# A hybrid encoder trunk on one core: experts gathered in pairs from split halves, the router per token tile, and identity products in TensorE's gaps

## The chip, the cores and the metric

The kernel runs on one core of one Trainium2 chip. The metric is the device time of one execution in microseconds (us), and a kernel's time is the median of its runs. The profile is one more execution, with its own time.

## The reference

The input is 256 tokens of 1024 float32 values. After a layer norm come two layers. Each is a token mixer (retention, S5, Hyena and mLSTM head groups), a residual and a norm, then a SwiGLU channel mixer, a residual and a norm. The channel mixer is dense in the first layer; in the second each token goes to the best two of eight experts:

```python
def moe_swiglu(x, router, w1, w3, w2):
    logits = (xt @ router).astype(jnp.float32)
    top_val, top_idx = lax.top_k(logits, TOP_K)      # TOP_K = 2 of N_EXPERTS = 8
    gate = jax.nn.softmax(top_val, axis=-1)
    combine = jnp.einsum("tk,tke->te", gate, jax.nn.one_hot(top_idx, N_EXPERTS))
    ...
    # out = sum over experts e of combine[:, e] * swiglu(xt, w1[e], w3[e], w2[e])
```

An expert has 3584 hidden columns (`w1`, `w3`: 1024 x 3584, `w2`: 3584 x 1024), so the weights of all eight are 352 MB and are read once.

## The kernel before, in words

The program is written out by hand for each engine. Semaphores tie the engines together, and each engine works in the order of its text. The tokens are two tiles of 128 (`h[:, t, :]`). The order around the change is: token mixer of layer 1 (`mix_1`), `layer_norm(3)` on DVE, transposes of the normed `h` on PE (`transposes_of_h(3)`, tile 1 first) into `hT` (ACT, `evacuate_h`), the router, the experts, `layer_norm(4)` and the output.

**Layer norm.** DVE computes the mean and variance of a tile, GpSimd (POOL) the power -1/2 (L500), DVE scales (L1484, L1490). PE stands still from the last product of the mixer until the first tile is normed.

**Router.** PE waits until all of `hT` is there, makes the logits (L1022, 16 products of 8 columns), DVE selects the best two (L2019 to L2035), PE counts places with products against a triangle and against ones (L1027 to L1031), and DVE turns them into `posx`, the place of each token in each expert's list of up to 128 tokens (L2044 to L2047).

**Experts.** One after the other, each in 14 chunks (`NC_E`) of 256 hidden columns, 112 chunks in all. Chunk `g` has 2 MB of `w1`, `w3` and 1 MB of `w2`, in a ring of four slots that SyncE (SP) fills: it issues the load of `w1`, `w3` (L374) when PE has finished `up` of the chunk that had the slot, and that of `w2` (L378) after `down`. The products are made from float32 data split into a high and a low part of the type fp32r (hi*hi, lo*hi, hi*lo; `SPLIT`). For a chunk ACT writes the high half of the weights (`split_up`, L1353, two pieces into one buffer `ex_up_hi`; L1449 for `w2`), DVE the low half (`up_lo`, L1962; `w2_lo`, L2086), PE makes `up` (L1075, 24 products of 512 columns), two transposes and `down` of the chunk before (L1096, 12 products of 512).

**An expert's tokens.** `prepare` (DVE, L2052) writes the one-hot matrix `pick_x`; `gather` (PE, L1039) multiplies `h`, plain float32, by it, 16 products of 128 columns in two halves, for one expert; `take_x` (ACT, L1408) and `x_lo` (DVE, L2069) split the result into `ex_x`, of which there are two. `placing` (L1046) transposes `pick_x` for the way back, `scatter` (L1059) and `add` (L2063) bring the result to the tokens. For expert x+1 this is done during chunks 7 to 11 of expert x: DVE writes `pick_x` in its chunk 7, PE gathers after chunks 8 and 9, `add` for the expert before is in DVE's chunks 4 and 6. Of a float32 product that is no transpose the trace has two records; of an fp32r product and of a transpose it has one.

A branch repeats all experts if one has more than 128 tokens; it isn't taken in the profile.

## Time and profile before

| | |
|---|---|
| median of 3 runs | 1730.88 us (1726.97 to 1731.34) |
| the profiled execution: its time, its span | 1726.48 us, 1724.6 us |
| PE matmul busy | 1650.9 us, 96% |
| DVE busy | 1353.5 us, 78% |
| ACT busy | 944.0 us, 55% |
| POOL busy | 56.4 us, 3% |
| mean granted TensorE clock | 0.958 |
| chain that ended last, by engine | PE 84%, DVE 10%, ACT 4% |

The clock is a share of 2.4 GHz; it is granted at 1.00 (2.4 GHz) or 0.50 (1.2 GHz). "PE L1075" is TensorE's matmul at line 1075. The experts are the stretch from 709.9 to 1707 us.

### The profile page before, as it was taken

What the parts mean: (1) busy time and instruction counts of PE and PEld (TensorE: products, weight loads), DVE (VectorE), ACT (ScalarE), POOL (GpSimd) and SP (SyncE); (2) the same over time, 40 slices, a digit from 0 to 9 for tenths busy, and PEclk for the clock granted to TensorE, in tenths of its full rate; (3) what the DMA queues carried; (4) which work ended last, traced back from release to release, by engine and by line L of the source; (5) the groups of instructions that cost most, each with busy time, mean ns of one, the idle gap of its engine ahead of it and who ended that gap; (6) DMA issues with size and microseconds to landing.
All of it is one profiled execution on the core that took longest, in us unless ns stands there. A gap on an engine that the chain in (4) does not pass through costs nothing.

```text
span 1724.6 us, 18678 instructions
## 1 busy us (share of the span) xinstructions
PE 1650.9 (96%) x7674; PEld 1306.7 (76%) x7674; DVE 1353.5 (78%) x1443; ACT 944.0 (55%) x943; POOL 56.4 (3%) x39
## 2 busy tenths in 40 slices
PE   6998989999999998899999999999999999999995
PEld 4665748988858764788888888888888888888883
DVE  6879456765665945598898998888988989888996
ACT  4312315654310232477777776777777767777772
POOL 0111000000011100000000000000000000000000
PEclk9978989999998978799999999999999999999997
DMA  7221152743433114598988998998989989989870
GB/s 311 98 98 49 74 212 86 270 182 147 173 145 147 49 73 182 208 371 344 375 351 339 372 353 346 366 362 337 364 348 354 361 356 356 360 330 374 350 305 26
DMA packets 40459, 444.23 MB, mean 258 GB/s; under 512 B 4400, under 2 KB 4528, under 8 KB 7216
## 3 DMA queue, kind: packets, MB, share of 16 engines
q1 hardware_dynamic: 39216, 438.78, 65.2%
q10 hardware_dynamic: 1152, 4.19, 0.6%
q8 instruction: 62, 1.02, 0.2%
q14 instruction: 29, 0.24, 0.0%
HBM read 437.71 MB, written 5.24 MB: 257 GB/s over the span
## 4 chain that ended last, share of the span: by engine, by line
PE 84%; DVE 10%; ACT 4%; issue 1%; DMA 0%; DVEq 0%; SPq 0%; ACTq 0%
PE bank L1075 33%; PE bank L1096 15%; PE bank L981 7%; PE bank L583 4%; PE bank L990 3%; PE bank L800 3%; PE bank L587 3%; PE bank L1039 2%; PE bank L753 1%; PE bank L1083 1%; DVE ring_lo L1962 1%; DVE ring_lo L2086 1%; ACT ex_up_hi L1353 1%; PE bank L726 1%; PE bank L1059 1%
## 5 line engine op out<-in xcount | busy, mean ns | idle before, releaser
L1962 DVE TENSOR_TENSOR ring_lo<-ring,ex_up_hi 128x2048 fp32r<-128x2048 f32 x224 | 512.8, 2290 | 50.9 <-ACT ex_up_hi L1353 50.7
L1353 ACT ACTIVATE ex_up_hi<-ring 128x2048 fp32r<-128x2048 f32 x224 | 429.1, 1916 | 115.7 <-PE bank L1075 108.0
L1075 PE MATMUL bank<-ex_up_hi,ex_x_hi 128*128 128x512 f32 x896 | 363.0, 405 | 3.7 <-DVE ring_lo L1962 3.7
L1075 PE MATMUL bank<-ring_lo,ex_x_hi 128*128 128x512 f32 x896 | 350.6, 391 | 0.0
L1075 PE MATMUL bank<-ex_up_hi,ex_x_lo 128*128 128x512 f32 x896 | 349.7, 390 | 0.0
L2086 DVE TENSOR_TENSOR ring_lo<-ring,ex_w_hi 128x2048 fp32r<-128x2048 f32 x112 | 255.5, 2282 | 1.4 <-ACT ex_w_hi L1449 1.4
L1449 ACT ACTIVATE ex_w_hi<-ring 128x2048 fp32r<-128x2048 f32 x112 | 213.4, 1905 | 0.0
L1075 PEld LDWEIGHTS bank<-ex_up_hi,ex_x_hi 128*128 128x128 f32 x896 | 168.3, 188 | 40.9 <-DVE ring_lo L1962 10.8
L1075 PEld LDWEIGHTS bank<-ring_lo,ex_x_hi 128*128 128x128 f32 x896 | 168.2, 188 | 36.2
L1075 PEld LDWEIGHTS bank<-ex_up_hi,ex_x_lo 128*128 128x128 f32 x896 | 168.8, 188 | 30.5
L1096 PE MATMUL bank<-ex_w_hi,ex_mid_hi 128*128 128x512 f32 x448 | 174.4, 389 | 2.1 <-DVE ex_mid_lo L2080 2.1
L1096 PE MATMUL bank<-ring_lo,ex_mid_hi 128*128 128x512 f32 x448 | 174.3, 389 | 0.0
L1096 PE MATMUL bank<-ex_w_hi,ex_mid_lo 128*128 128x512 f32 x448 | 174.3, 389 | 0.0
L981 PE MATMUL bank<-ff_x_hi,ff_up_hi 128*128 128x256 f32 x352 | 102.1, 290 | 3.5 <-DVE ff_up_lo L1968 3.5
L981 PE MATMUL bank<-ff_x_lo,ff_up_hi 128*128 128x256 f32 x352 | 100.7, 286 | 0.0
L981 PE MATMUL bank<-ff_x_hi,ff_up_lo 128*128 128x256 f32 x352 | 100.6, 286 | 0.0
L1096 PEld LDWEIGHTS bank<-ex_w_hi,ex_mid_hi 128*128 128x128 f32 x448 | 84.1, 188 | 19.7 <-DVE ring_lo L2086 2.3
L1096 PEld LDWEIGHTS bank<-ring_lo,ex_mid_hi 128*128 128x128 f32 x448 | 84.1, 188 | 17.5
L1096 PEld LDWEIGHTS bank<-ex_w_hi,ex_mid_lo 128*128 128x128 f32 x448 | 84.1, 188 | 17.4
L2080 DVE TENSOR_TENSOR ex_mid_lo<-bank,ex_mid_hi 128x256 fp32r<-128x256 f32 x112 | 47.4, 424 | 61.5 <-ACT ex_mid_hi L1419 61.5
L583 PE MATMUL bank<-hT,win 128*128 128x256 f32 x384 | 88.9, 391 | 2.2 <-ACT hT L1146 1.5
L1444 ACT ACTIVATE sc<-bank 128x256 f32<-128x256 f32 x112 | 43.0, 384 | 86.1 <-PE bank L1075 86.1
(316 smaller groups left out, 2187.7 us busy)
## 6 DMA issues: line engine op xcount, KB each, us to landing
ring<-moe SPq DMA_DIRECT2D x112, 2048.0 KB, 7.6
ring<-moe SPq DMA_DIRECT2D x112, 1024.0 KB, 7.6
ring<-ffn SPq DMA_DIRECT2D x11, 3072.0 KB, 10.9
win<-w_in SPq DMA_DIRECT2D x12, 2048.0 KB, 8.6
win<-w_out SPq DMA_DIRECT2D x4, 2048.0 KB, 10.4
lnb<-ln SPq DMA_DIRECT2D x4, 1024.0 KB, 6.1
tab<-yT ACTq DMA_DIRECT2D x8, 512.0 KB, 5.6
pr<-par SPq DMA_DIRECT2D x2, 1728.0 KB, 12.2
```

The costliest lines, as they stand in the source:

```text
L583: ins = mm(b[:, q * L:(q + 1) * L], w[:, k, c:c + P], hT[:, k, :], start=(k == 0), stop=(k == KT - 1))
L587: ins = mm(b[:, :], hT[:, k, part * P:(part + 1) * P], w[:, k, :], start=(k == 0), stop=(k == KT - 1))
L800: ins = mm(bank[b][:, :], yT[:, k, t * P:(t + 1) * P], w[:, k, :], start=(n == 0 and i == 0), stop=(n == 3 and i == 1))
L981: ins = mm(bank[4 + u % 2][:, w * L:(w + 1) * L], ff_up[j][:, w, k, :], ff_x[i][:, k, :], start=(k == 0 and n == 0), stop=(k == KT - 1 and ...
L990: ins = mm(bank[2 * t + hf][:, :], ff_mid[i][:, u % 2, t * P:(t + 1) * P], ff_w2[j][:, hf * 512:(hf + 1) * 512], start=False, stop=(u == N ...
L1075: ins = mm(b[:, :], ex_x[x % 2][x_][:, k, :], (ex_up_hi, lo)[w_][:, k, :], start=(k == 0 and m == 0), stop=(k == KT - 1 and m == 2))
L1096: ins = mm(bank[2 * (x % 2) + hf][:, :], ex_mid[a][:, g % 2, f * P:(f + 1) * P], w2[b], start=(c == 0 and f == 0 and m == 0), stop=(c == N ...
L1353: act(ex_up_hi[:, HS * q:HS * (q + 1), :], wt[:, HS * q:HS * (q + 1), :], ACT.Copy).then_inc(e_uh, 1)
L1449: act(ex_w2_hi[g % 2][:, :], ring[here][:, UPW:SLOT], ACT.Copy).then_inc(e_wh, 1)
L1962: tt(ring_lo[s][:, half], ring[s][:, half], hi.bitcast(F32), ALU.subtract).then_inc(e_ul, 1)
L2080: tt(ex_mid[1][:, g % 2, :], bank[4 + g % 2][:, 0:L], ex_mid[0][:, g % 2, :].bitcast(F32), ALU.subtract).then_inc(e_mid, 1)
L2086: tt(ring_lo[s][:, UPW:SLOT], ring[s][:, UPW:SLOT], ex_w2_hi[g % 2][:, :].bitcast(F32), ALU.subtract).then_inc(e_wl, 1)
```

## The change

1. **Gather in pairs, split.** `pick_x` holds the one-hot matrices of two experts (256 columns). `h` is split beforehand into `h_hi` (ACT, in `keep_h`) and `h_lo` (POOL, L511 of the changed kernel), both fp32r, and a gather for a pair is 32 products of 256 columns in four quarters of 8. `ex_x` gets a third buffer. For the pair of experts x+1, x+2 (x odd) DVE writes `pick_x` in chunk 6, PE gathers after chunks 7 to 10, ACT and DVE split in chunks 8 to 11 in pieces of 256 columns. The first pair is gathered half before and half inside the first `up`.
2. **Router.** The logits of a tile are made as soon as its half of `hT` is there; the comparisons are written over both tiles at once; the gates and the test for more than 128 tokens come after the first `prepare`; the places are released before the totals. `h` times alpha, the start value of `acc`, is made per tile next to `h_hi`.
3. **Identity products.** `keep_busy(n, bank)` issues n products of the identity with itself (float32, 128 columns, so two records each) into a PSUM bank that nobody uses then: 10 before the first transposes, 18 before those of norm 1, 22 before and 6 between those of norm 3, and 4, 12 and 6 in the router.
4. The load of the last norm's weights (`load_ln(4)`) moves behind expert 5 on SP, since `ex_x2` lies over `lnb`.

```diff
@@ ex_x, h_hi, h_lo, pick_x
-                for i, a in enumerate(("cv", "pr"))]
+                for i, a in enumerate(("cv", "pr", "lnb"))]
+        h_hi = [over_sb("h_hi0", "yT", D, [P, D]), over_sb("h_hi1", "cst", CONST["pos"][0], [P, D])]
+        h_lo = over_sb("h_lo", "h", 0, [P, TT, D])
-        pick_x = over_sb("pick_x", "sc", 1024, [P, TT, P])
+        pick_x = over_sb("pick_x", "sc", 1024, [P, TT, 2 * P])
@@ gpsimd, after the norm's powers
+                if n == 3:
+                    for i, t in enumerate(TILES[n]):
+                        po.wait_ge(q_res, i + 1)
+                        po.wait_ge(q_hi, i + 1)
+                        nc.gpsimd.tensor_tensor(h_lo[:, t, :], h[:, t, :], h_hi[t][:, :].bitcast(F32), ALU.subtract
+                                                ).then_inc(q_lo, 1)
@@ tensor
+            def keep_busy(count, b):
+                for _ in range(count):
+                    mm(bank[b][:, 0:P], ident, ident, start=True, stop=True)
@@ transposes_of_h
                 for i, t in enumerate(TILES[n]):
+                    if n == 3 and i:
+                        keep_busy(6, 7)
                     pe.wait_ge(h_ready, 2 * n + i + 1)
@@ the order of PE's text
             pe.wait_ge(s_id, 16)
+            keep_busy(10, 7)
             transposes_of_h(0)
             mix_0()
+            keep_busy(18, 7)
             transposes_of_h(1)
             dense()
             transposes_of_h(2)
             mix_1()
+            keep_busy(22, 7)
             transposes_of_h(3)
-            pe.wait_ge(ht_ready, 16)
-            for t in range(TT):
+            for i, t in enumerate(TILES[3]):
+                if i:
+                    keep_busy(4, 4)
                 for k in range(KT):
+                    if k % HS == 0:
+                        pe.wait_ge(ht_ready, 12 + 2 * i + k // HS + 1)
                     ins = mm(bank[6][:, t * NE:(t + 1) * NE], hT[:, k, t * P:(t + 1) * P], rw[:, k, :], ...
             ins.then_inc(q_lg, 1)
+            keep_busy(12, 4)
             pe.wait_ge(q_sel, 1)
...
+            keep_busy(6, 4)
-            def gather(x, q):
-                pe.wait_ge(e_p, x + 1)
-                for i in range(4):
-                    k = 4 * q + i
+            def gather(m, q):
+                if q == 0:
+                    pe.wait_ge(e_p, m + 1)
+                elif q >= 2:
+                    pe.wait_ge(e_xg, 4 * m + q - 1)
+                for i in range(2):
+                    k = 2 * q + i
                     for t in range(TT):
-                        ins = mm(bank[6 + q][:, i * P:(i + 1) * P], h[:, t, k * P:(k + 1) * P],
-                                 pick_x[:, t, :].bitcast(F32), start=(t == 0), stop=(t == 1))
+                        for n, part in enumerate((h_hi[t], h_lo[:, t, :])):
+                            ins = mm(bank[6 + q % 2][:, i * 2 * P:(i + 1) * 2 * P], part[:, k * P:(k + 1) * P],
+                                     pick_x[:, t, :], start=(t == 0 and n == 0), stop=(t == 1 and n == 1))
@@ up
                     for k in range(HS * q, HS * (q + 1)):
+                        if g % CH == 0 and k in (2, 4):
+                            gather(x // 2, k // 2 + 1)
@@ scalar
+            def keep_h(t):
+                act(h_hi[t][:, :], h[:, t, :], ACT.Copy).then_inc(q_hi, 1)
+                act(acc[:, t, :], h[:, t, :], ACT.Copy, scale=ALPHA).then_inc(q_res, 1)
@@ evacuate_h
+                    if n == 3 and i:
+                        keep_h(TILES[3][0])
@@ vector
+            def prepare(m):
+                e = 2 * m % NE
+                tt(pick_x[:, :, :].rearrange("p t (i s) -> p t i s", i=2), bc(bc(K("iota"), 1, 2), 1, TT),
+                   bc(posx[:, :, e:e + 2], 3, P), ALU.is_equal).then_inc(e_p, 1)
@@ DVE's chunks (x odd)
-                        if c == 7:
+                        if c == 6:
                             ve.wait_ge(e_tm, x + 1)
-                            prepare(x - x0 + 1)
-                        if c in (9, 10):
-                            x_lo(x + 1, c - 9)
+                            prepare((x + 1) // 2)
+                        if 8 <= c < 12:
+                            x_lo((x + 1) // 2, c - 8)
```

PE's order from the transposes of norm 3 to the first expert, before: `cst,h` is a transpose of `h`, `pr,hT` the router, `vo,cst` the counting of places, `pick_x,h` the gather.

```order
L514 MATMUL bank<-cst,h 128x128 x16
L1022 MATMUL bank<-pr,hT 128x8 x16
L1027 MATMUL bank<-vo,cst 128x8
L1028 MATMUL bank<-vo,cst 128x8
L1029 MATMUL bank<-vo,cst 128x8
L1030 MATMUL bank<-vo,cst 128x8
L1031 MATMUL bank<-vo,cst 128x8
L1039 MATMUL bank<-pick_x,h 128x128 x16
```

And in the changed kernel, where L522 is the identity product and L1068 the gather:

```order
L522 MATMUL bank<-cst 128x128 x22
L532 MATMUL bank<-cst,h 128x128 x8
L522 MATMUL bank<-cst 128x128 x6
L532 MATMUL bank<-cst,h 128x128 x8
L1045 MATMUL bank<-pr,hT 128x8 x8
L522 MATMUL bank<-cst 128x128 x4
L1045 MATMUL bank<-pr,hT 128x8 x8
L522 MATMUL bank<-cst 128x128 x12
```

Both tiles' transposes stand ahead of the first router products, and the 4 and 12 identity products stand between and behind the router's; 6 more stand between the counting and the gather.

DVE's order over chunk 6 and 7 of an odd expert, before (`ret` is `add`, `ring_lo<-ring,ex_up_hi` half of the next chunk's low weights):

```order
L2086 TENSOR_TENSOR ring_lo_68<-ring,ex_w_hi_58 128x2048
L2063 SCALAR_TENSOR_TENSOR ret<-bank,vo,ret 128x512 x2
L1962 TENSOR_TENSOR ring_lo_66<-ring,ex_up_hi 128x2048
L2121 TENSOR_TENSOR sc<-sc,bank 128x256
L1962 TENSOR_TENSOR ring_lo_66<-ring,ex_up_hi 128x2048
L2080 TENSOR_TENSOR ex_mid_lo<-bank,ex_mid_hi 128x256
L2086 TENSOR_TENSOR ring_lo_65<-ring,ex_w_hi_57 128x2048
L2052 TENSOR_SCALAR pick_x<-cst,vo 128x128 x2
```

And in the changed kernel:

```order
L2132 TENSOR_TENSOR ring_lo_66<-ring,ex_w_hi_58 128x2048
L2106 SCALAR_TENSOR_TENSOR ret<-bank,vo,ret 128x512 x2
L2095 TENSOR_TENSOR pick_x<-cst,vo 128x512
L2009 TENSOR_TENSOR ring_lo_68<-ring,ex_up_hi 128x2048
L2171 TENSOR_TENSOR sc<-sc,bank 128x256
```

The one-hot matrix, now 512 columns in one instruction, has moved into the chunk that also has `add`, ahead of the low weights that PE takes next.

## Rows read from the trace of the kernel before

**Rows 1.** The page: PE's busy time, and the DMA engines' busy tenths in 40 slices

```profile
PE 1650.9 (96%) x7674; PEld 1306.7 (76%) x7674; DVE 1353.5 (78%) x1443; ACT 944.0 (55%) x943; POOL 56.4 (3%) x39
...
DMA  7221152743433114598988998998989989989870
```

**Rows 2.** Groups by line, 590 us to the end: count | busy us, mean ns | idle before <-releaser

```profile
L1353 ACT ACTIVATE ex_up_hi<-ring 128x2048 fp32r<-128x2048 f32 x224 | 429.1, 1916 | 115.7 <-PE bank L1075 108.0 <-PE bank L800 7.7
L1075 PE MATMUL bank<-ex_up_hi,ex_x_hi 128*128 128x512 f32 x896 | 363.0, 405 | 3.7 <-DVE ring_lo L1962 3.7
...
L1039 PE MATMUL bank<-pick_x,h 128*128 128x128 f32 x256 | 33.4, 288 | 1.4 <-DVE pick_x L2052 1.4
...
L2069 DVE TENSOR_TENSOR ex_x_lo<-bank,ex_x_hi 128x512 fp32r<-128x512 f32 x16 | 11.0, 685 | 6.2 <-ACT ex_x_hi L1408 6.2
...
L1408 ACT ACTIVATE ex_x_hi<-bank 128x512 fp32r<-128x512 f32 x16 | 9.5, 593 | 9.2 <-PE bank L1039 9.2
```

**Rows 3.** SP's issues in expert 1, one at the end of each chunk's `up`

```profile
898.54 0.33 SPq L374 DMA_DIRECT2D ring<-moe  x1
...
906.95 0.33 SPq L374 DMA_DIRECT2D ring<-moe  x1
...
917.16 0.33 SPq L374 DMA_DIRECT2D ring<-moe  x1
```

**Rows 4.** Timeline of PE in the dense stage: start us, length us

```profile
300.07 0.28 PE L981 MATMUL bank<-ff_x_hi,ff_up_hi 128*128 128x256 f32 x1
300.19 0.28 PE L981 MATMUL bank<-ff_x_lo,ff_up_hi 128*128 128x256 f32 x1
```

**Rows 5.** Timeline of DVE in chunk 6 of expert 1

```profile
888.86 1.40 DVE L2063 SCALAR_TENSOR_TENSOR ret<-bank,vo,ret 128x512 f32<-128x512 f32 x2
890.18 2.28 DVE L1962 TENSOR_TENSOR ring_lo<-ring,ex_up_hi 128x2048 fp32r<-128x2048 f32 x1
```

**Rows 6.** Timeline of PE: the first product of chunk 7 of expert 1

```profile
892.55 0.46 PE L1075 MATMUL bank<-ex_up_hi,ex_x_hi 128*128 128x512 f32 x1
```

**Rows 7.** Timeline of all engines, norm 3 to the second chunk [idle before <-releaser]

```profile
687.75 4.49 DVE L1962 TENSOR_TENSOR ring_lo<-ring,ex_up_hi 128x2048 fp32r<-128x2048 f32 x2
...
690.54 6.99 PE L1022 MATMUL bank<-pr,hT 128*128 128x8 f32 x32 [0.69 <-ACT hT L1146]
697.57 0.17 DVE L2019 COPY vo<-bank 128x16 f32<-128x16 f32 x1 [5.34 <-PE bank L1022]
...
699.13 0.29 DVE L2031 TENSOR_TENSOR vo<-vo 128x128 f32<-128x128 f32 x1
...
703.74 6.18 PE L1039 MATMUL bank<-pick_x,h 128*128 128x128 f32 x32 [1.38 <-DVE pick_x L2052]
...
714.92 1.28 ACT L1444 ACT_TABLE_LOAD   x1
...
720.78 0.49 PE L1075 MATMUL bank<-ex_up_hi,ex_x_hi 128*128 128x512 f32 x1 [0.23 <-DVE ring_lo L1962]
```

**Rows 8.** Timeline of all engines: a subtraction on DVE beside an addition on POOL

```profile
144.16 2.35 POOL L493 TENSOR_TENSOR ring<-ring 128x1024 f32<-128x1024 f32 x1 [8.32 <-DVE ring L1818]
...
145.50 1.56 DVE L1645 TENSOR_TENSOR lnb<-lnb 128x512 f32<-128x512 f32 x1
```

**Rows 9.** Stretches: length, busy (count) of PE, PEld, DVE, ACT, POOL, PEclk, DMA

```profile
679.90:684.80 4.90, 0.05 (x1) 0.00 (x0) 4.76 (x9) 3.71 (x2) 1.49 (x2) 1.00 0.82 291
...
690.50:697.60 7.10, 6.99 (x32) 6.90 (x32) 1.76 (x2) 0.00 (x0) 0.00 (x0) 0.50 0.99 420
```

**Rows 10.** Stretch of the same view in the mixer of layer 1

```profile
548.30:551.70 3.40, 3.40 (x19) 3.40 (x18) 0.00 (x0) 0.33 (x1) 0.00 (x0) 0.50 1.01 429
```

**Rows 11.** Timeline of PE: products of 16 columns in the mixer of layer 1

```profile
543.93 3.73 PE L593 MATMUL bank<-pr,hT 128*128 128x16 f32 x32
```

**Rows 12.** Timeline of PE and DVE at norm 1

```profile
255.03 1.97 PE L514 MATMUL bank<-cst,h 128*128 128x128 f32 x8 [5.29 <-DVE h L1490]
...
260.44 1.29 DVE L1985 TENSOR_TENSOR ff_x_lo<-bank,ff_x_hi 128x512 fp32r<-128x512 f32 x2 [0.48 <-ACT ff_x_hi L1146]
```

More of the change, by code:

```diff
@@ L445, in _ @@
                 load_first(c)
-            load_ln(4)
             def load_chunk(g):
@@ L1033, in gather @@
-            def gather(x, q):
-                pe.wait_ge(e_p, x + 1)
-                for i in range(4):
-                    k = 4 * q + i
+            mm(bank[5][:, 0:NE], K("before"), sel[:, 0, :], start=True, stop=True)
+            mm(bank[5][:, NE:2 * NE], K("ones"), sel[:, 0, :], start=True, stop=False)
+            mm(bank[5][:, NE:2 * NE], K("before"), sel[:, 1, :], start=False, stop=True).then_inc(q_pos, 1)
+            mm(bank[3][:, 0:NE], K("ones"), sel[:, 0, :], start=True, stop=False)
@@ L1105, in all_experts @@
                 x0 = b * NE
-                gather(x0, 0)
-                gather(x0, 1)
-                placing(x0)
+                pe.wait_ge(q_lo, TT)
+                for q in range(2):
+                    gather(x0 // 2, q)
                 for i in range(CH):
@@ L1427, in all_experts @@
                         split_up(q, MOE_SLOTS[CH % SLOTS])
-                take_x(x0, 0)
-                take_x(x0, 1)
+                for q in range(4):
+                    take_x(x0 // 2, q)
                 for i in range(CH):
@@ L1436, in all_experts @@
                         mid_hi(g - 1)
-                    if c in (9, 10) and x < x0 + NE - 1:
-                        take_x(x + 1, c - 9)
+                    if 8 <= c < 12 and x % 2 and x < x0 + NE - 1:
+                        take_x((x + 1) // 2, c - 8)
                     if more:
@@ L2017, in _ @@
             ve.wait_ge(q_lg, 1)
-            ve.wait_ge(mix_ready, 4)
             link(nc.vector.tensor_copy(lg, bank[6][:, 0:16].rearrange("p (t e) -> p t e", t=2)))
+            other, own = bc(lg, 2, NE), bc(lg, 3, NE)
+            tt(cmp1, other, own, ALU.is_gt)
+            link(tt(cmp2, other, own, ALU.is_equal))
+            link(tt(cmp2, cmp2, bc(K("lower").rearrange("p (a b) -> p a b", a=NE), 1, TT), ALU.mult))
+            link(tt(cmp1, cmp1, cmp2, ALU.add))
+            link(nc.vector.tensor_reduce(rt[3], cmp1, AX.X, ALU.add))
@@ L2020, in _ @@
+            ts(sel, rt[3], 1.5, None, ALU.is_lt).then_inc(q_sel, 1)
+            ve.wait_ge(q_sel, 1)
+            ts(rt[4], sel, -4096.0, 4096.0, ALU.mult, ALU.add)
             link(nc.vector.tensor_reduce(rt1[:, 0:2], lg, AX.X, ALU.max))
             tt(el, lg, bc(rt1[:, 0:2], 2, NE), ALU.subtract).then_inc(q_l, 1)
-            for t in range(TT):
-                a, b = bc(lg[:, t, :], 1, NE), bc(lg[:, t, :], 2, NE)
-                tt(cmp1[:, t], a, b, ALU.is_gt)
-                ins = tt(cmp2[:, t], a, b, ALU.is_equal)
@@ L2027, in _ @@
-            link(ins)
-            for t in range(TT):
-                ins = tt(cmp2[:, t], cmp2[:, t], K("lower").rearrange("p (a b) -> p a b", a=NE), ALU.mult)
-            link(ins)
-            link(tt(cmp1, cmp1, cmp2, ALU.add))
-            for t in range(TT):
-                ins = nc.vector.tensor_reduce(rt[3][:, t, :], cmp1[:, t], AX.X, ALU.add)
-            link(ins)
-            ts(sel, rt[3], 1.5, None, ALU.is_lt).then_inc(q_sel, 1)
-            ve.wait_ge(q_sel, 1)
-            ve.wait_ge(q_ex, 1)
@@ L2047, in _, with gates_and_total @@
-            tt(posx[:, :, 0:NE], rt[4], bank[7][:, 0:16].rearrange("p (t e) -> p t e", t=2), ALU.add).then_inc(q_px, 1)
+            tt(posx[:, :, 0:NE], rt[4], bank[5][:, 0:16].rearrange("p (t e) -> p t e", t=2), ALU.add).then_inc(q_px, 1)
             ve.wait_ge(q_px, 1)
-            def prepare(e):
-                for t in range(TT):
-                    ins = ts(pick_x[:, t, :], K("iota"), posx[:, t, e:e + 1], None, ALU.is_equal)
-                ins.then_inc(e_p, 1)
+            def gates_and_total():
+                ve.wait_ge(q_ex, 1)
+                link(tt(el, el, sel, ALU.mult))
+                link(nc.vector.tensor_reduce(rt1[:, 2:4], el, AX.X, ALU.add))
+                link(nc.vector.reciprocal(rt1[:, 4:6], rt1[:, 2:4]))
+                link(tt(comb[:, :, 0:NE], el, bc(rt1[:, 4:6], 2, NE), ALU.mult))
+                ve.wait_ge(q_pos, 2)
+                link(nc.vector.tensor_reduce(rt1[:, 6:7], bank[3][:, 0:NE], AX.X, ALU.max))
+                ts(over[:, 0:1], rt1[:, 6:7], P + 0.5, None, ALU.is_gt).then_inc(q_px, 1)
+                ve.wait_ge(q_px, 2)
@@ L2093, in all_experts @@
                         up_lo(CH, q, MOE_SLOTS[CH % SLOTS])
-                prepare(0)
-                x_lo(x0, 0)
-                x_lo(x0, 1)
-                placed(x0)
+                prepare(x0 // 2)
+                if not b:
+                    gates_and_total()
+                for q in range(4):
+                    x_lo(x0 // 2, q)
                 for i in range(CH):
```

92 lines of the change are left out of this document (51 added, 41 removed).

## The prediction

> **What bounds the kernel now.** I read the page first. PE is busy 96% of the span, DVE 78%, and the DMA engines stand at eight or nine tenths through the experts [rows 1], so three engines are near their ends and a share alone doesn't say which binds. Next the groups by line. ACT's split waits 108 us for PE; PE's `up` waits 3.7 us in all for DVE's low halves, over 112 chunks [rows 2]. So the experts are PE's own work, and what a PE instruction costs there comes back in full. SP's issues give the length of a chunk: 898.54 to 906.95 is 8.41 us, and with a gather, 906.95 to 917.16, it is 10.21 us [rows 3]. At 3 MB per chunk the loads are delivered at that pace, and nobody waits for one: no DMA stands among the releasers of the costly groups [rows 2].
>
> Then the timeline from norm 3 to the second chunk. Here nothing overlaps: router products for 6.99 us, DVE's selection, counting, one-hot, gather for 6.18 us, and the second half of chunk 1 not before 720.78 [rows 7]. The stretches show why the products are slow: the clock was 1.00 while PE stood still before the transposes, and 0.50 in the router [rows 9].
>
> **Gathers in the expert loop.** A half gather costs 10.21 - 8.41 = 1.80 us, an expert 3.60 us. Seven are in the loop (experts 1 to 7): 25.2 us. A product of 256 columns of fp32r starts 0.12 us after the one before, each with new weights, in the dense stage [rows 4]. That is the shape of the new gather. Before, 16 float32 records of 0.107 us would be 1.71, so 0.09 of the 1.80 is the switch. A quarter gather is 8 x 0.12 + 0.09 = 1.05 us, a pair 4.2 us, and three pairs are in the loop: 12.6 us. **Gain 12.6 us.** Bounds: at 0.107 per product three pairs are 11.4 us (gain 13.8); with 0.15, more than the row by a quarter, 15.5 us (gain 9.7).
>
> The splits stay beside PE. ACT pays 0.593 for 512 and 1.916 for 2048 columns, so by that line 0.37 us for 256; DVE by 0.685 and 2.29 pays 0.42 [rows 2]. Two of each per quarter are 0.75 and 0.84, against 0.59 and 0.69 of before, in a chunk that PE needs 9.5 us for. Placing and scatter are unchanged in number.
>
> **What is late next: DVE's chunk 6.** DVE has `add` at 888.86 for 1.40 us and the low half at 890.18 for 2.28, so it ends at 892.46; PE takes it at 892.55 [rows 5, 6]. There is 0.1 us to spare. The one-hot matrix of a pair, 512 columns, now stands ahead of that half; by the 512-column row it is 0.69 us [rows 2]. PE waits 0.6 us, in experts 1, 3 and 5; before, the chunk after was 0.1 us longer itself, since the one-hot stood there. **Loss 3 x 0.5 = 1.5 us**, between 0 (if PE's idle moment is made up by its own order) and 2.1.
>
> **Router.** In steps, with the times of before's trace.
> - Logits. Both tiles' `hT` is needed, as before, but PE is now ahead: at high clock products of few columns cost 3.73 / 32 = 0.117 us a record [rows 11], at low 6.99 / 32 = 0.218 [rows 7]. Transposes of the second tile end near 688.8, then 16 records, 8 of identity, 16 records: 693.4 at high clock, 697 with everything low; 697.5 before.
> - The way to the selection. DVE has 4.49 us of low halves from 687.75 [rows 7]. POOL gets two subtractions of 128x1024 with both inputs in SBUF. Here is the place that I chose most about. A POOL operation of that size took 2.35 us, and DVE's L1645, two SBUF inputs, took 1.56 us starting at 145.50 and ending just after POOL did (146.51), where 512 columns otherwise take 0.69 [rows 8, 2]. So they exclude each other. POOL's first input is ready near 689, inside DVE's 4.49 us. The two engines then need 4.49 + 2 x 2.35 = 9.2 us one after the other: 687.75 + 9.2 = 697.0, and the comparisons start there, whichever goes first, though the logits were ready earlier.
>
> The Trainium skill, "SBUF — State Buffer", section "Who interferes with whom", says that a DVE instruction with two SBUF inputs contends with a GpSimd instruction that reads SBUF and that the loser fully blocks. The trace agrees, 1.56 for 0.69 us. By that rule the router gains the 3.0 us below; without it 6.3.
>
> - Selection: seven operations, five of them over 128 columns at 0.29 us [rows 7], about 1.8 us with the links: 698.8.
> - Counting: five products at 0.22 to 0.44 us (two records each), of which DVE needs three; then the place (0.2) and one-hot 0.69, beside them 6 identity products, 1.3 us high or 2.6 low. The gather starts at 701.3 at high clock, 703.6 at low, against 703.74 [rows 7].
> - From the gather to chunk 1's second half. First quarter 0.96, its split 1.9 with the hand-overs, then in `up` 6 products, a quarter, 6 products, a quarter: (12 x 0.227) + 1.92 = 4.6. The last split on ACT ends 8.3 us after the start; the next weights' first high half 1.92 [rows 2]; from the start of the table load to the second half 720.78 - 714.92 = 5.86 as before [rows 7]. Together 16.1 us, against 720.78 - 703.74 = 17.04.
>
> So the second half comes at 717.4 (high) or near 720.5 (low, with slower quarters). 12 identity products after the logits are 2.6 us high, so PE is quiet again for 1 to 3 us until the counting; I take mostly high: **gain 3.0 us**. Upper bound: POOL and DVE don't exclude each other, DVE is free at 692.24, and the gather starts at 698.4: gain 6.3. Lower bound: the clock is low from the transposes on; then logits at 698.5, twelve products 5.2 us, counting 2.2, six products 2.6, gather at 708.5, that is 4.7 us lost.
>
> What speaks for that bound is this trace: 32 products of 16 columns kept PE busy for 3.73 us at high clock [rows 11], and the stretch right behind was granted 0.50 though PE was busy 3.40 of 3.40 us [rows 10]. [...]
>
> **Norms.** At norm 1 PE is idle 5.29 us before the transposes [rows 12], at norm 3 about as long [rows 9]; 18 products are 36 x 0.107 = 3.9 us, 22 are 4.7 us, at the high clock that the stretch before has [rows 9]. Both fit. At norm 1 DVE waited 0.48 us for ACT at 260.44 and was busy before it [rows 12], so faster transposes give at most that: 0.4. At norm 3 it is in the router's sum. At the start ten products run while DVE norms; DVE and ACT set the pace there, 0.3, between 0 and 1 (half of a 1.97 row [rows 12]). **Gain 0.7 us.** If the clock were low at norm 3, 22 products would be 9.6 us and 4.3 us late.
>
> The load moved on SP has 200 us to land; it costs nothing, and would cost its few us only if SP reached it after the last chunk.
>
> **Sum.** 12.6 - 1.5 + 3.0 + 0.7 = 14.8 us, about 1711.7 from the profiled 1726.48. That execution is 4.4 us below the median of the three; from the median, 1730.88 - 14.8 = **1716 us**.
>
> **The rivals.**
> 1. The router gives nothing or costs: the clock falls, the identity products stand ahead of ready work. Gain 12.6 - 1.5 + 0.7 - (0 to 4.7) = 7 to 12: 1719 to 1724. [...] Chance 0.18.
> 2. The router gives its full 6.3 and DVE's chunk 6 costs nothing: 12.6 + 6.3 + 0.7 = 19.6: 1711. For it: PE's waits before sum to only 3.7 us [rows 2]; against it [rows 8]. Chance 0.14.
> 3. The experts lose their PE bound: at 8.41 us a chunk for longer runs, DVE (3 x 2.29 + 2 x 0.42 = 7.7 us of work a chunk) or the loads (3 MB in 8.41 us, 374 GB/s) hold it, and half of the loop's gain goes: 1722. Against it: that pace was held before, and PE's waits sum to 3.7 us [rows 2, 3]. Chance 0.05.
> 4. Slower. The gather's products run at the float32 price: 256 columns would be two records of twice 0.107, 0.43 us. A pair is then 32 x 0.43 + 4 x 0.09 = 14.1 us against 7.2, 17 us more for the loop's seven experts (42.3 against 25.2) and about 5 more at the start: 1730.88 + 17 + 5 + 1.5 - 0.7 = 1754. It decides from 0.12 + 14.8 / 128 = 0.24 us a product, over the 128 gather products. Against it: both operands are fp32r, as in [rows 4]. Chance 0.02.
>
> My forecast has 0.61: 1712 to 1720. The range that leaves about 0.15 out takes in rival 2 and most of rival 1 and 3, and a median that moves by 4 us as before's runs did: 1706 to 1723. A measurement of this kernel can tell about 0.3% (5.2 us) from no change, so faster begins below 1725.7: all cases but 4 and the far end of 1 and 3. Faster 0.93, same 0.04, slower 0.03.
>
> **What would show it.** SP's issues in an odd expert: four chunks of about 9.5 us (7 to 10) and none of 10.2; in an even one no gather. 128 gather records 0.12 apart. Between 689 and 697 POOL's two subtractions end to end with DVE's, one of them stretched; PE's wait before chunk 7 of experts 1, 3 and 5 near 0.6 us. The clock at 1.00 from norm 3 to the router's first half. The prediction is wrong if quarters cost over 1.2 us, if the gather starts before 699 or after 705, or if PE waits for DVE elsewhere in the loop.

## The result, and the profile after

The changed kernel takes 1715.3 us, the median of 4 runs (1714.37 to 1717.69), against 1731.09 us (4 runs, 1726.97 to 1731.34) for the kernel before. The ratio is 0.9919, with a 95% interval of 0.9902 to 0.9935. By this ratio it is faster by 0.8%, that is 14 us, 11 to 17 by the interval; the two medians are 15.8 us apart.

The profiled executions have spans of 1724.6 and 1714.0 us, 10.6 apart. The rest of the difference of the medians lies in runs of before that have no trace. Nine runs of the kernel before on another chip went from 1722.56 us at a mean clock of 0.961 to 1731.19 at 0.956, so it moves by itself by more than half the gain. What follows explains the 10.6 us. I cut both spans at six events that both traces have:

| stretch | before | after | gain | forecast |
|---|---|---|---|---|
| start to the end of mixer 0 | 249.15 | 250.03 | -0.88 | 0.3 |
| norm 1, to the first dense product | 12.63 | 12.06 | 0.57 | 0.4 |
| dense stage and mixer of layer 1, to the mixer's end | 417.58 | 418.08 | -0.50 | 0 |
| mixer's end to the end of norm 3 | 8.47 | 8.47 | 0 | 0 |
| norm 3 to the second half of chunk 1 | 32.95 | 31.78 | 1.17 | 3.0 |
| from there to the start of the last chunk | 967.82 | 956.61 | 11.21 | 11.1 |
| last chunk, last norm, output | 35.98 | 37.01 | -1.03 | 0 |
| sum | 1724.6 | 1714.0 | 10.6 | 14.8 |

The page after: engines' shares, and PE's `up` with its idle time before it (compare [rows 1, 2]).

```profile
PE 1652.5 (96%) x7702; PEld 1306.3 (76%) x7702; DVE 1358.0 (79%) x1443; ACT 946.4 (55%) x962; POOL 64.0 (4%) x41
...
L1109 PE MATMUL bank<-ex_up_hi,ex_x_hi 128*128 128x512 f32 x896 | 362.5, 405 | 5.1 <-DVE ring_lo L2009 4.7
```

PE's busy time did not fall, although the gathers became cheaper: 78 identity products (156 records) were added. The busy share can't show this change. The wait for DVE's low halves went from 3.7 to 4.7 us.

**The expert loop.** SP's issues in expert 1, after: start us, length us. L377 is the load of `w1`, `w3` at the end of each chunk's `up`.

```profile
895.36 0.33 SPq L377 DMA_DIRECT2D ring<-moe  x1
...
904.77 0.33 SPq L377 DMA_DIRECT2D ring<-moe  x1
...
914.16 0.33 SPq L377 DMA_DIRECT2D ring<-moe  x1
...
923.55 0.33 SPq L377 DMA_DIRECT2D ring<-moe  x1
```

The issues behind a quarter gather are 9.39 to 9.41 us apart, where a half gather made 10.21 [rows 3]. PE's timeline in chunk 8, first and last of a quarter's eight products:

```profile
907.29 0.28 PE L1068 MATMUL bank<-pick_x,h_hi 128*128 128x256 f32 x1
907.41 0.28 PE L1068 MATMUL bank<-pick_x,h_lo 128*128 128x256 f32 x1
...
908.13 0.28 PE L1068 MATMUL bank<-pick_x,h_lo 128*128 128x256 f32 x1
```

They start 0.12 us apart, so a quarter costs 0.98 to 1.0 us. DVE's timeline in chunk 6 of the same expert, and PE's at the start of chunk 7:

```profile
885.07 1.40 DVE L2106 SCALAR_TENSOR_TENSOR ret<-bank,vo,ret 128x512 f32<-128x512 f32 x2
886.39 0.69 DVE L2095 TENSOR_TENSOR pick_x<-cst,vo 128x512 fp32r<-128x512 f32 x1
886.99 2.29 DVE L2009 TENSOR_TENSOR ring_lo<-ring,ex_up_hi 128x2048 fp32r<-128x2048 f32 x1
```

```profile
888.51 0.39 PE L1130 MATMUL bank<-ring_lo,ex_mid_hi 128*128 128x512 f32 x1
889.34 0.50 PE L1109 MATMUL bank<-ex_up_hi,ex_x_hi 128*128 128x512 f32 x1 [0.44 <-DVE ring_lo L2009]
```

The one-hot matrix takes 0.69 us ahead of the low half, and PE's next product starts 0.83 us after the last one where 0.23 is the pace: 0.6 us lost. SP's issues show it in all three odd experts that prepare a pair: this one chunk is 9.15, 9.11 and 9.08 us long in experts 1, 3 and 5, where it was 8.52 in expert 1 before.

**The router.** Timeline of all engines, after, from norm 3 to the gather [idle before <-releaser]; against [rows 7]:

```profile
688.56 6.65 DVE L2009 TENSOR_TENSOR ring_lo<-ring,ex_up_hi 128x2048 fp32r<-128x2048 f32 x2
...
689.63 1.85 PE L1045 MATMUL bank<-pr,hT 128*128 128x8 f32 x16
...
689.80 7.62 POOL L511 TENSOR_TENSOR h_lo<-h,h_hi 128x1024 fp32r<-128x1024 f32 x2 [3.39 <-ACT ret L1182]
...
692.31 1.85 PE L1045 MATMUL bank<-pr,hT 128*128 128x8 f32 x16
...
694.02 2.92 PE L522 MATMUL bank<-cst 128*128 128x128 f32 x24
695.14 0.16 DVE L2065 COPY vo<-bank 128x16 f32<-128x16 f32 x1
695.33 2.24 DVE L2067 TENSOR_TENSOR vo<-vo 128x128 f32<-128x128 f32 x1
697.49 0.28 DVE L2068 TENSOR_TENSOR vo<-vo 128x128 f32<-128x128 f32 x1
...
699.01 0.39 PE L1051 MATMUL bank<-vo,cst 128*128 128x8 f32 x2 [2.07 <-DVE vo L2072]
...
700.35 0.69 DVE L2095 TENSOR_TENSOR pick_x<-cst,vo 128x512 fp32r<-128x512 f32 x1
...
700.81 2.91 PE L522 MATMUL bank<-cst 128*128 128x128 f32 x12
...
703.37 0.56 PE L1068 MATMUL bank<-pick_x,h_hi 128*128 128x256 f32 x1
```

Read it in three steps. The 32 router records now take 3.7 us and are done near 694.1 (before: 6.99 us, copy at 697.57). Then the logits wait: DVE's low halves take 6.65 us instead of 4.49, because POOL's subtractions run beside them, and DVE's first comparison, that takes 0.28 us for its neighbour L2068, takes 2.24 and ends when POOL does. One by one, the low halves took 2.28 and 4.45 us and the subtractions, 2.35 us alone, took 3.26 and 4.39: each figure is what comes out if whole instructions of the two engines take turns. Last, the one-hot matrix is there at 701.04, and the gather starts 2.33 us later, since six identity products stand in front of it. The stretches of the clock (length, busy and count of PE, PEld, DVE, ACT, POOL, then the granted clock):

```profile
686.00:699.40 13.40, 11.06 (x96) 10.68 (x96) 13.12 (x15) 5.84 (x8) 8.03 (x3) 1.00 0.84 356
699.40:706.30 6.90, 6.90 (x35) 6.90 (x35) 1.91 (x10) 0.87 (x3) 0.00 (x0) 0.51 0.00 0
```

The clock was at 2.4 GHz until 699.4, behind PE's 2.07 us of standing still, and at 1.2 GHz then, in the counting, the six identity products and the first half of the gather.

### The profile page after: what moved, and what is told of

Its sections match the earlier page's. It is cut to its first block, busy times and chain, and to the rows that moved or that the text cites. A ratio compares the mean times of both kernels' runs of the same rounds, so it can differ in the third digit from the quotient of the medians.

```text
span 1714.0 us, 18765 instructions
## 1 busy us (share of the span) xinstructions
PE 1652.5 (96%) x7702; PEld 1306.3 (76%) x7702; DVE 1358.0 (79%) x1443; ACT 946.4 (55%) x962; POOL 64.0 (4%) x41
## 3 DMA queue, kind: packets, MB, share of 16 engines
q8 instruction: 63, 1.03, 0.2%
## 4 chain that ended last, share of the span: by engine, by line
PE 82%; DVE 12%; ACT 4%; issue 1%; DMA 1%; SPq 0%; DVEq 0%; ACTq 0%
PE bank L1109 33%; PE bank L1130 15%; PE bank L999 7%; PE bank L601 4%; PE bank L1008 3%; PE bank L818 3%; PE bank L605 3%; DVE ring_lo L2009 2%; PE bank L771 1%; DVE ring_lo L2132 1%; PE bank L1117 1%; ACT ex_up_hi L1398 1%; PE bank L744 1%; PE bank L1091 1%; PE bank L1068 1%
## 5 line engine op out<-in xcount | busy, mean ns | idle before, releaser
L605 PE MATMUL bank<-win,hT 128*128 128x512 f32 x192 | 87.9, 612 | 0.0
## 6 DMA issues: line engine op xcount, KB each, us to landing
ring<-ffn SPq DMA_DIRECT2D x11, 3072.0 KB, 10.2
```

Source lines behind the costliest of these rows:

```text
L605: ins = mm(b[:, :], hT[:, k, part * P:(part + 1) * P], w[:, k, :], start=(k == 0), stop=(k == KT - 1))
```

## The experiments

Each run is timed beside the kernel before on its own chip, and the ratio is to those runs. Two kernels whose intervals overlap are not told apart by their times; there the profiles carry the reading, and the text says so. "Router" is the stretch of the table from the end of norm 3 to the second half of chunk 1. The diffs are against the changed kernel unless said.

| kernel | median us (n) | ratio, 95% | router |
|---|---|---|---|
| changed kernel | 1715.3 (4) | 0.9919 [0.9902, 0.9935] | 31.78 |
| e1 no identity products | 1715.36 (4) | 0.9926 [0.9906, 0.9946] | 30.20 |
| e2 one-hot after the low half | 1713.28 (4) | 0.9909 [0.9893, 0.9926] | 31.78 |
| e3 first low halves late | 1713.54 (4) | 0.9911 [0.9894, 0.9928] | 31.04 |
| e4 without the six | 1714.69 (4) | 0.9920 [0.9903, 0.9936] | 30.19 |
| e5 pairs in float32 | 1721.18 (4) | 0.9954 [0.9938, 0.9970] | 29.03 |
| e6 kernel before with identity products | 1724.86 (10) | 0.9974 [0.9963, 0.9986] | 30.02 |
| e7 combined | 1708.70 (5) | 0.9892 [0.9877, 0.9908] | 27.14 |
| e8 combined, no identity products | 1713.79 (6) | 0.9914 [0.9899, 0.9929] | 30.34 |
| e9 subtractions on DVE | 1709.44 (4) | 0.9889 [0.9865, 0.9912] | 27.17 |
| e10 combined, subtractions on DVE | 1706.64 (5) | 0.9876 [0.9857, 0.9895] | 26.14 |
| e11 without the ten | 1714.80 (4) | 0.9923 [0.9901, 0.9946] | 31.96 |

### e1: no identity products

```diff
-                    if n == 3 and i:
-                        keep_busy(6, 7)
...
-            keep_busy(10, 7)
...
-            keep_busy(18, 7)
...
-            keep_busy(22, 7)
...
-                if i:
-                    keep_busy(4, 4)
...
-            keep_busy(12, 4)
...
-            keep_busy(6, 4)
```

> All identity products are left out; pairs, split and router order stay. Theory (DVE and POOL taking turns sets the router's time): DVE's selection starts as late as in the changed kernel, about 9.2 us after the second tile's norm, the gather starts sooner by the 2.9 us of the six products that stood before it but runs at 0.50, and the whole is 1713 to 1718 us. Rival (the high clock carries the gain of norms and router): the logits come 3 us later than DVE is free, and the whole is 1719 us or more.

The time is that of the changed kernel, within what the intervals can tell (about 0.2% each way, 3 to 4 us). Timeline of e1, the router's products and the copy of the logits:

```profile
693.70 6.84 PE L1038 MATMUL bank<-pr,hT 128*128 128x8 f32 x32
...
700.58 0.17 DVE L2056 COPY vo<-bank 128x16 f32<-128x16 f32 x1 [2.12 <-PE bank L1038]
```

The router's products are slow again, 6.84 us, yet the router is 1.6 us shorter than in the changed kernel. POOL and DVE are all but through by the time that the logits come, and nothing stands before the gather. Norm 3, on the other hand, ends at 691.88 instead of 688.64. Of these 3.2 us, 2.1 arise at norm 1, where the 18 products are missing (14.1 us against 12.06 to the first dense product, with the clock low in part of it), and 1.4 in the stretch up to the end of the mixer of layer 1, which has no identity products in either kernel. So not all of it is theirs; e4, e6 and e8 look at the parts.

### e2: the one-hot matrix behind the low half

```diff
-                        if c == 6:
-                            ve.wait_ge(e_tm, x + 1)
-                            prepare((x + 1) // 2)
...
                     if more:
                         up_lo(g + 1, 0, after)
+                    if c == 6 and x % 2 and x < x0 + NE - 1:
+                        ve.wait_ge(e_tm, x + 1)
+                        prepare((x + 1) // 2)
```

> In DVE's chunk 6 of experts 1, 3 and 5 the one-hot matrix is written behind the first low half instead of ahead of it. Theory: PE's wait before chunk 7 (0.6 us) goes in all three, 1.5 to 1.8 us in the span, and chunk 7 is not longer. Rival: the wait moves to the second half of chunk 7 or to w2, and the span is the same within 0.3 us.

DVE's timeline in chunk 6 of expert 1, e2:

```profile
886.22 2.28 DVE L2009 TENSOR_TENSOR ring_lo<-ring,ex_up_hi 128x2048 fp32r<-128x2048 f32 x1
888.41 0.69 DVE L2095 TENSOR_TENSOR pick_x<-cst,vo 128x512 fp32r<-128x512 f32 x1
```

Chunk 6 is 8.43 us long instead of 9.00, chunk 7 9.63 instead of 9.50, each from the first product of its `up` to that of the next. So 0.44 us an odd expert and 1.3 in all come back, nearly what the chunk-6 term lost and a little less than the 1.5 to 1.8 expected, since chunk 7 did get 0.13 us longer. The median is 2 us lower; the intervals overlap, so the chunk lengths carry this verdict.

### e3: the first low halves behind the selection

```diff
-            for q in range(2):
-                up_lo(0, q, MOE_SLOTS[0])
             ve.wait_ge(q_lg, 1)
...
                 prepare(x0 // 2)
                 if not b:
                     gates_and_total()
+                    for q in range(2):
+                        up_lo(0, q, MOE_SLOTS[0])
```

> The two low halves of chunk 0 (4.5 us on DVE) are made behind the gates instead of ahead of the selection. Theory (turns of DVE and POOL): the comparisons start when POOL's second subtraction ends, 2.5 us sooner, the clock stays high through the counting, and the gather starts 3 to 4 us sooner; 3 us in all. Rival (the router products and identity products on PE set it): the gather starts at most 1 us sooner.

Timeline of e3, POOL and DVE, and PE's first product of the first `up`:

```profile
689.84 2.35 POOL L511 TENSOR_TENSOR h_lo<-h,h_hi 128x1024 fp32r<-128x1024 f32 x1 [3.39 <-ACT ret L1182]
...
692.70 2.35 POOL L511 TENSOR_TENSOR h_lo<-h,h_hi 128x1024 fp32r<-128x1024 f32 x1 [0.51 <-ACT ret L1182]
...
694.24 0.17 DVE L2063 COPY vo<-bank 128x16 f32<-128x16 f32 x1 [5.55 <-PE bank L1045]
694.44 0.75 DVE L2065 TENSOR_TENSOR vo<-vo 128x128 f32<-128x128 f32 x1
...
704.91 0.47 PE L1109 MATMUL bank<-ex_up_hi,ex_x_hi 128*128 128x512 f32 x1 [3.57 <-DVE ex_x_lo L2112]
```

With no DVE instruction beside it a subtraction takes POOL 2.35 us; in the changed kernel the two took 7.62. The logits are copied as soon as they are there, the gather starts at 699.19 instead of 703.37, and the clock is still at 1.00 there. But the gain is only 0.7 us at the router's end, not the 3 expected. The low halves now stand ahead of the split of the gathered tokens, so PE waits 3.57 us before the first `up`, and from the gather's start to there it is 5.72 us instead of 3.76. Then chunk 0 takes 11.32 us instead of 9.79: the clock is at 1.2 GHz from 706.2 to 709.6, inside it. The stall moved, and the low clock with it.

### e4: without the six products before the gather

```diff
-            keep_busy(6, 4)
```

> Only the six identity products ahead of the gather are left out. Theory (they stand ahead of ready work at 0.50): the gather starts 2.3 us sooner; it runs at 0.50 for longer, 0.8 us, and so do the products behind it, so 0.5 to 1.5 us are gained. Rival (they keep the gather fast): the first quarters take 1.7 us each and the first up runs at 0.50 too, and the span is the same or up to 1 us longer.

Timeline of e4, the one-hot matrix and the first gather product:

```profile
700.94 0.69 DVE L2094 TENSOR_TENSOR pick_x<-cst,vo 128x512 fp32r<-128x512 f32 x1
...
701.78 0.55 PE L1067 MATMUL bank<-pick_x,h_hi 128*128 128x256 f32 x1 [0.23 <-DVE pick_x L2094]
```

The gather follows the one-hot matrix after 0.15 us instead of 2.33, and the router is 1.6 us shorter, as long as in e1. The first gather product runs 0.55 us, at 1.2 GHz, and so it did with the six (0.56), so they did not hold the clock. Of the 2.2 us by which the gather starts sooner after norm 3, 0.6 are lost again, since more of the gather now runs at the low clock: 17.69 us from its start to the router's end instead of 17.05. The net cost of the six is 1.6 us, as the expectation had it (0.5 to 1.5) and a little more. In the median 0.6 us is too little to tell.

### e5: pairs, but the products in float32

```diff
-                for n, part in enumerate((h_hi[t], h_lo[:, t, :])):
-                    ins = mm(bank[...], part[:, k * P:(k + 1) * P], pick_x[:, t, :], ...)
+                ins = mm(bank[...], h[:, t, k * P:(k + 1) * P], pick_x[:, t, :].bitcast(F32), ...)
```
`h_hi` and `h_lo`, and so POOL's subtractions, are gone; the sums are the same.

> Pairs are gathered as in the changed kernel, but from h in float32: 16 products of 256 columns (two records each), no h_hi, no h_lo, no subtractions on POOL. Theory (the gain in the loop is the fp32r price, 0.12 us a product, and not the pairing): a quarter is 8 records of 0.213 us, 1.8 us, so chunks 7 to 10 of experts 1, 3 and 5 are 10.2 us each and the loop loses about 9 us against the changed kernel; the router wins about 2 us, since POOL no longer holds DVE's comparisons; 1721 to 1724 us. Rival (fewer, wider instructions are the gain): 1715 us or less.

SP's issues in expert 1, e5:

```profile
891.60 0.33 SPq L377 DMA_DIRECT2D ring<-moe  x1
...
901.77 0.33 SPq L377 DMA_DIRECT2D ring<-moe  x1
...
911.94 0.33 SPq L377 DMA_DIRECT2D ring<-moe  x1
```

A chunk with a quarter is 10.17 us, 1.76 more than 8.41: a pair then costs 7.0 us, as two experts did before (7.2). So pairing alone brings almost nothing, and the loop's gain is the price of the fp32r products of 256 columns. Whether the split would give it without the pairs, in products of 128 columns, was not run. The kernel is 6 us slower than the changed one, less than the 9.2 us that twelve quarters lose, since the router is 2.75 us shorter without POOL's subtractions.

### e6: the kernel before with identity products

```diff
@@ against the kernel before
+                    if n == 3 and i:
+                        keep_busy(6, 7)
...
+            keep_busy(10, 7)
             transposes_of_h(0)
...
+            keep_busy(18, 7)
             transposes_of_h(1)
...
+            keep_busy(22, 7)
             transposes_of_h(3)
```

> The kernel before with the identity products of the norms alone (10, 18, 22 and 6), nothing else changed. Theory: DVE's chain sets norms 1 and 3, so the stretches behind them end within 0.5 us of before, less the 2 to 3 us that warm transposes and router products give if the clock holds there; 1727 to 1731 us. Rival (the clock matters): 4 us or more faster, below 1726.

It is 3.8 us faster than the kernel before, 2.4 to 6.4 by the interval. My theory of 1727 to 1731 us fell; the time is the rival's (below 1726), though just short of its 4 us. Timeline of e6:

```profile
688.47 5.43 PE L1032 MATMUL bank<-pr,hT 128*128 128x8 f32 x32 [0.74 <-ACT hT L1156]
...
700.12 5.61 PE L1049 MATMUL bank<-pick_x,h 128*128 128x128 f32 x32 [1.38 <-DVE pick_x L2062]
```

The transposes and the first half of the router's products run at the high clock (it falls at 690.2; 5.43 us against 6.99), and the router is 2.9 us shorter. In the old kernel nobody stands between the logits and the selection, so that gain gets through.

### e7 and e8: both repairs of the order, with and without identity products

e7 is the changed kernel with e2 and e4, and on DVE only the first low half before the selection:

```diff
-            for q in range(2):
-                up_lo(0, q, MOE_SLOTS[0])
+            up_lo(0, 0, MOE_SLOTS[0])
...
                     x_lo(x0 // 2, q)
+                    if q == 1 and not b:
+                        up_lo(0, 1, MOE_SLOTS[0])
```

> The changed kernel with the one-hot matrix behind the first low half in chunk 6, the second low half of chunk 0 made behind the second split of the gather instead of ahead of the selection, and without the six identity products before the gather. Theory: 1.3 us from chunk 6, and the comparisons start 1.5 to 2 us sooner, the gather 3.5 us sooner and the second half of chunk 1 near 3.5 us sooner, since no low half stands between the gather and its first split: 1709 to 1712 us. Rival (the start of the experts hangs on ACT's and DVE's own order, as the low halves behind the gates showed with 0.7 of 4.2 us): at most 2.5 us in all, 1713 us.

> The same as the combined kernel, without any identity product. Theory (they give nothing that can be measured here): within 1.5 us of the combined kernel. Rival (with DVE out of the way the router products at 0.50 set the time): logits 2.5 to 3 us later than DVE is free, and 3 us or more slower than the combined kernel.

e7 takes 1708.7 us; by the ratios it is 4.7 us below the changed kernel (0.0027 of 1730), though the intervals still overlap. In the profile the router is 4.6 us shorter. 1709 to 1712 was expected. The copy of the logits comes at 691.18, 5.6 us after norm 3 (6.5 in the changed kernel), the gather at 695.86, 10.2 us after (14.7). Here DVE's first comparison still takes 1.12 us beside POOL. And the clock falls in the gather, though PE hardly stood still before it. Stretches of e7 (length; busy of PE, PEld, DVE, ACT, POOL; clock):

```profile
690.00:696.00 6.00, 5.34 (x46) 5.09 (x46) 4.08 (x14) 0.22 (x1) 2.35 (x2) 1.00 0.68 289
696.00:699.50 3.50, 3.50 (x17) 3.24 (x17) 1.42 (x7) 0.69 (x3) 0.00 (x0) 0.51 0.00 0
```

Its longest idle time in the 6 us before was 0.63 us, ahead of the gather. So the 2.07 us of standing still in the changed kernel are not shown to be why the clock falls there.

e8 leaves the identity products out of e7 and takes 5.1 us more, in the same series (the slowest of e7's runs, 1712.46, is 0.4 above the fastest of e8's, so the size is uncertain by some 3 us). So here my expectation that they would be worth as little as in e1 fell, and the rival held. The router is 3.2 us longer. The rest lies ahead of it: in the profiles mixer 0 ends 3.3 us later in e8, and the stretch with the mixer of layer 1 is 2.1 us shorter, and neither can be put down to the products. The same products are worth nothing that can be measured when the turns of POOL and DVE hide the sooner logits and six stand before the gather, 3.8 us in the kernel before, and 5.1 when the turns are shorter.

### e9 and e10: POOL's subtractions on DVE

```diff
-                        nc.gpsimd.tensor_tensor(h_lo[:, t, :], h[:, t, :], h_hi[t]..., ALU.subtract)
...
             for q in range(2):
                 up_lo(0, q, MOE_SLOTS[0])
+            for i, t in enumerate(TILES[3]):
+                ve.wait_ge(q_res, i + 1)
+                ve.wait_ge(q_hi, i + 1)
+                tt(h_lo[:, t, :], h[:, t, :], h_hi[t][:, :].bitcast(F32), ALU.subtract).then_inc(q_lo, 1)
```

e9 has this alone, all identity products included; e10 has it and e7's order.

> The changed kernel with the two subtractions that make h_lo on DVE, behind its two low halves and ahead of the selection, and none on POOL. Theory (DVE and POOL exclude each other): DVE needs 4.5 us and twice 1.2 us where both engines in turns needed 9.2 us, so the comparisons start about 2 us sooner after norm 3 than in the changed kernel; the counting, six identity products and the gather follow, and the second half of chunk 1 comes 1.5 to 2.5 us sooner; 1713 to 1714 us. Rival (POOL's work ran beside DVE's, and DVE's own queue is what counts): 2.4 us more on DVE put the comparisons later, not sooner.

> The combined kernel with the two subtractions on DVE. Theory: DVE has 2.3 + 2.5 us to do before the logits are there, 8.5 us after norm 3's end less 3; the first comparison is no longer stretched (1.12 us against 0.29), the gather starts 0.8 us sooner after norm 3: 1707.5 to 1709 us. Rival: ACT's second copy of h comes too late for DVE and the subtraction stands ahead of the selection: the same as the combined kernel or slower.

Timeline of e9, from the low halves to the gather:

```profile
687.64 4.49 DVE L2003 TENSOR_TENSOR ring_lo<-ring,ex_up_hi 128x2048 fp32r<-128x2048 f32 x2
...
692.05 2.36 DVE L2061 TENSOR_TENSOR h_lo<-h,h_hi 128x1024 fp32r<-128x1024 f32 x2
...
694.32 0.17 DVE L2063 COPY vo<-bank 128x16 f32<-128x16 f32 x1
694.52 0.29 DVE L2065 TENSOR_TENSOR vo<-vo 128x128 f32<-128x128 f32 x1
...
697.39 1.58 PE L516 MATMUL bank<-cst 128*128 128x128 f32 x12
...
698.73 0.36 PE L1062 MATMUL bank<-pick_x,h_hi 128*128 128x256 f32 x1
```

DVE does both subtractions in 2.36 us where POOL needed 4.70, its low halves take 4.49 us again, and the comparison 0.29. DVE's whole work up to the comparisons is 6.9 us; shared with POOL it was 8.9 until the second comparison could start. PE stands still only 0.23 us before the counting, the clock stays at 1.00, and the six products cost 0.7 us instead of 2.3. The router takes 27.17 us, 4.6 less, and the kernel 1709.44. Expected were 1.5 to 2.5 us and 1713 to 1714: the comparisons do come 2 us sooner, as the theory had it, but what the high clock and the cheaper six give besides was left out. By the ratio (0.9889) this one edit gives as much as e7 (0.9892) with three. Its interval overlaps that of the changed kernel; against e11 in its own series, which is the changed kernel less ten products, every run of e9 is faster (1707.13 to 1710.21 against 1713.66 to 1715.30).

e10 is the best version here: 1706.64 us, ratio 0.9876 against 0.9919, with intervals that don't meet; 1707.5 to 1709 was expected. Its timeline, DVE's subtractions, the copy and the gather:

```profile
687.43 1.22 DVE L2059 TENSOR_TENSOR h_lo<-h,h_hi 128x1024 fp32r<-128x1024 f32 x1
...
689.28 1.23 DVE L2059 TENSOR_TENSOR h_lo<-h,h_hi 128x1024 fp32r<-128x1024 f32 x1 [0.64 <-ACT ret L1175]
...
690.86 0.17 DVE L2061 COPY vo<-bank 128x16 f32<-128x16 f32 x1 [0.35 <-PE bank L1039]
...
695.26 0.36 PE L1061 MATMUL bank<-pick_x,h_hi 128*128 128x256 f32 x1 [0.64 <-DVE pick_x L2091]
```

DVE now waits for PE's logits, not the other way round. The router is at 26.14 us, 5.6 less than in the changed kernel and 1.0 less than in e7, and the clock stays at 1.00 through all of it, where e7 had 3.4 us at the low clock. Which part of that 1.0 is the clock's was not separated.

### e11: without the ten products at the start

```diff
-            keep_busy(10, 7)
```

> The changed kernel without the ten identity products at the start. Theory (they raise the clock 9 us sooner and move the later stretches at 0.50, and the mixers' end doesn't come sooner): clock 1.00 from about 22 us instead of 13, DVE 0.5 to 1 us later at 35 us, and the end of mixer 0 within 1 us of the changed kernel; the same time within 1.5 us. Rival (a high clock at the start is a gain that lasts): 1 to 2 us slower at the end of mixer 0.

The median is the changed kernel's within 0.5 us. In the profile the clock rises at 24.4 us instead of 13.4, and mixer 0 ends at 251.69 instead of 250.03, as the rival had it (1 to 2 us later) and not the theory (within 1). But a later stretch, up to the end of the mixer of layer 1, is then 5.2 us shorter, and the two don't hang together by any instruction, so the gain is not seen in the time. This stretch in four kernels, from the last `up` product of the dense stage to the end of that mixer, the same instructions in each (length; busy of PE, PEld, DVE, ACT, POOL; clock). The changed kernel:

```profile
458.57:680.17 221.60, 215.88 (x846) 147.15 (x845) 137.17 (x234) 40.69 (x77) 24.31 (x14) 0.89 0.30 114
```
e1:
```profile
460.38:683.41 223.03, 217.54 (x846) 148.99 (x845) 137.24 (x234) 40.70 (x77) 24.31 (x14) 0.89 0.29 113
```
e10:
```profile
458.14:676.84 218.70, 212.79 (x846) 145.39 (x845) 137.12 (x234) 40.70 (x77) 24.31 (x14) 0.91 0.30 116
```
e11:
```profile
461.34:677.74 216.40, 211.09 (x846) 144.03 (x845) 137.15 (x234) 40.77 (x77) 24.31 (x14) 0.91 0.30 117
```

DVE's and ACT's times are equal, only PE's differ, with the clock. The stretch is between 216.4 and 223.0 us in the eight profiles read for it (also before, e6, e7 and e8). The kernel before had 219.92.

## Why the prediction was right, and where a step was not

The time (1715.3 against 1716), the sign and the range held, and the likeliest case came. By its steps:

**Gathers, gain 12.6: right.** The products start 0.12 us apart, a quarter costs 0.98 to 1.0 for 1.05 forecast, and the loop gives 11.21 us where 12.6 - 1.5 = 11.1 was the sum. e5 shows the cause: with float32 products in the same pairs and quarters the quarter chunks are 10.17 us and the gain is gone. Rival 4 (the float32 price per product) is excluded by the changed kernel itself. Rival 3 also fell: PE waits only 1.0 us more for DVE's low halves, all groups of the loop taken together, and the chunks without a gather kept their 8.41.

**DVE's chunk 6, loss 1.5: right.** PE stood 0.6 us where it was said, and e2 gives 1.3 us back. The loop's sum is as good as it is because two small misses meet: a quarter was cheaper by 0.05 to 0.07 us, twelve times, and chunk 6 lost 0.6 us each time instead of 0.5.

**Router, gain 3.0: too large, 1.17 measured.** Its step on POOL and DVE was right: 9.2 us one after the other from 687.75 was the forecast, and they took 8.9 us from 688.56 to POOL's end at 697.42; the comparisons got going at 697.5.

The Trainium skill, "SBUF — State Buffer", section "Who interferes with whom", has a DVE instruction with two SBUF inputs and a GpSimd instruction that reads SBUF exclude each other, and the loser fully blocked. The trace agrees: the comparison, both inputs in SBUF, took 2.24 us for 0.28 and ended with POOL's subtraction.

The step that failed is the next one, "12 identity products after the logits are 2.6 us high, so PE is quiet again for 1 to 3 us until the counting; I take mostly high". PE was quiet for 2.07 us, and the clock fell, at 699.4. The prediction had the low case worked out: gather at 703.6, second half of chunk 1 near 720.5. The trace has 703.37 and 720.42, but part of this nearness is luck: the forecast times count from a norm 3 that ends at 687.83, and it ended at 688.64. From norm 3 the gather came after 14.7 us (high case 13.5, low case 15.8) and the second half after 31.8 (29.6 and 32.7), so the run lies between the two, closer to the low one. From the gather to the second half it took 17.05 us, not 16.1 (16.16 in e9, all at 2.4 GHz), since the first quarters ran at the low clock. In that case six identity products are 2.9 us in front of ready work; without them e4 is 1.6 us shorter. That the clock fell because PE was quiet is argued, not shown: in e9 there was neither the wait nor the low clock, but e7 had a low stretch without such a wait.

**Where rival 2's 6.3 us were.** e9 has them: take the turns away and the router gives 32.95 - 27.17 = 5.8 us, and e10 gives 6.8. So the bound was well sized, and the exclusion, with the low clock that came behind its wait and was absent in e9, was what stood between.

**Norms, gain 0.7: norm 1 right, the start wrong, the idea too narrow.** Norm 1 gave 0.57 for 0.4. At the start the sign is wrong in the profile (-0.88), and e11 finds the ten products worth nothing that can be measured in the time. As a price of the identity products together the 0.7 was misleading: most of what can be put down to them is in the router, 2.9 us in e6 and 3.2 from e8 to e7, and there it depends on what else waits. In the changed kernel as it stands they are worth nothing that can be measured (e1).

**Not in the sum.** The start, the mixers and the end of the kernel move by one or two us each way with low-clock stretches. Together they took 2.4 us of the profiled difference (-0.88, -0.50, -1.03). The forecast from the median met 1715.3 within a microsecond with some luck: the profiled gain is 10.6 for 14.8, and the profiled execution of before was 4.4 us below its median.

What stays open: why the low stretches of the mixers, and the one in e7's gather, lie where they do, and so whether the identity products have a part in that. Whether 12 products after the logits are the right number was not tried.

## What to carry to other kernels

When a helper's work goes to an idle engine, look at which engine runs beside it at that moment: POOL was 97% idle, and moving 4.7 us of work there cost the critical path more than the 2.4 us that it takes on DVE itself. Filler products, meant to keep the clock up, paid here only where the work behind them was not ready and what they made sooner was waited for; test them again after each repair, since their worth went from nothing measurable to about 5 us with the order around them. Split products pay by the price of one product, which the trace shows for the same shape elsewhere; pairing alone brought 0.2 us a pair here.
